# First attention of a two-layer encoder step: where queries and keys are turned and split

## What is computed

```python
h = rmsnorm(x, norm_mix[0])
z = h @ w_in                       # 1024 -> 3 * 1024 + 16
q, k, v = 16 heads of 64 each      # k and v are outputs too
logf = log_sigmoid(z[..., 3072:] + b_f)
cum = cumsum(logf)                 # per head, along the tokens
logits = q @ k.T * 64 ** -0.5 + cum_q[:, None] - cum_k[None, :]
p = softmax(where(mask, logits, NEG))
x = x + (p @ v) @ w_o
x = x + square(relu(rmsnorm(x) @ w_up)) @ w_down
```

## Time and profile before

| | |
|---|---|
| median of 3 runs | 1616.43 us (1614.15 to 1616.51) |
| the profiled execution's own time | 1614.33 us |
| its span in the profile | 1612.5 us |
| PE busy in the span | 1534.1 us, 95% |
| DVE, ACT, POOL busy | 1083.9, 734.0, 411.6 us |
| projection of the first layer | to 195.24 us |
| first attention | 195.24 us to about 372 us |

### The profile page before, as it was taken

One profiled execution on the slowest core, in us unless ns is written; L12 is line 12 of the kernel. 1 busy time (PEld: TensorE's weight loads), 2 busy tenths in 40 slices (PEclk: granted clock), 3 DMA queues, 4 the chain that ended last, 5 costly groups with the idle time before them and its releaser, 6 DMA issues.

```text
span 1612.5 us, 30906 instructions
## 1 busy us (share of the span) xinstructions
PE 1534.1 (95%) x10817; PEld 1447.4 (90%) x10817; DVE 1083.9 (67%) x1997; ACT 734.0 (46%) x1528; POOL 411.6 (26%) x435
## 2 busy tenths in 40 slices
PE   7999889999899999999988897999989999999997
PEld 6777679989899999999988686999888999999997
DVE  5221067875987777787674246788598878778775
ACT  5232157774443434334253434777444433434434
POOL 0010045552332222122000003455343222212200
PEclk9999979999999999999999898999999999999998
DMA  8253531200222312313230537221012322321311
GB/s 286 93 188 90 158 98 40 63 27 27 77 73 87 104 54 102 104 52 104 71 113 2 205 130 213 67 66 33 27 52 79 105 82 75 104 97 59 104 52 60
DMA packets 127780, 146.06 MB, mean 91 GB/s; under 512 B 17776, under 2 KB 103984, under 8 KB 127712
## 3 DMA queue, kind: packets, MB, share of 16 engines
q1 hardware_dynamic: 127712, 145.16, 28.2%
HBM read 120.54 MB, written 24.60 MB: 90 GB/s over the span
## 4 chain that ended last, share of the span: by engine, by line
PE 81%; issue 7%; DVE 6%; ACT 3%; DMA 1%; POOL 1%; SPq 0%; POOLq 0%; ACTq 0%; DVEq 0%
PE ps L2058 25%; PE ps L1745 23%; PE ps L2089 20%; PE ps L1916 3%; PE ps L1960 2%; PE ps L1961 2%; PE ps L1962 2%; PE ps L1931 1%; PE ps L1887 1%; PE ps L1939 1%; DVE wul L1471 1%; DVE wul L1266 1%; PE ps L1909 1%; DVE bl L1517 1%; DVE xT L1500 1%
## 5 line engine op out<-in xcount | busy, mean ns | idle before, releaser
L1569 DVE TENSOR_TENSOR xT<-xT,ps 128x592 f32<-128x592 f32 (+1 forms) x256 | 195.0, 762 | 55.2 <-PE ps L2058 53.3
L2089 PE MATMUL ps<-bh,wuh 128*128 128x296 f32 (+1 forms) x512 | 153.9, 301 | 8.5 <-DVE wul L1471 4.9
L755 POOL TENSOR_TENSOR prob<-prob,rs 128x144 f32<-128x144 f32 (+4 forms) x160 | 118.8, 756 | 140.0 <-DVE rs L1370 140.0
L2089 PE MATMUL ps<-bl,wuh 128*128 128x296 f32 (+1 forms) x512 | 153.6, 300 | 0.0
L2089 PE MATMUL ps<-bh,wul 128*128 128x296 f32 (+1 forms) x512 | 153.3, 299 | 0.0
L1380 DVE TENSOR_TENSOR ptl<-ps,pth 128x256 fp32r<-128x256 f32 (+2 forms) x192 | 95.9, 501 | 66.0 <-ACT pth L989 65.9
L1745 PE MATMUL ps<-wh,xgh 128*128 128x512 f32 (+5 forms) x320 | 123.2, 385 | 4.1 <-DVE zr L1668 3.2
L822 POOL TENSOR_TENSOR ssum<-raw 128x512 f32<-128x512 f32 x32 | 49.2, 1538 | 292.3 <-DMA raw<-in_w_up 289.8
L1745 PE MATMUL ps<-wl,xgh 128*128 128x512 f32 (+5 forms) x320 | 122.0, 381 | 0.0
L1745 PE MATMUL ps<-wh,xgl 128*128 128x512 f32 (+5 forms) x320 | 121.4, 380 | 0.0
L2058 PE MATMUL ps<-hh,dn2h 128*128 128x296 f32 (+1 forms) x512 | 111.3, 299 | 0.0
(11 more groups left out here) (261 smaller groups left out, 4686.6 us busy)
## 6 DMA issues: line engine op xcount, KB each, us to landing
raw<-in_w_up SPq DMA_DIRECT2D x32, 1024.0 KB, 7.1
raw<-in_w_down SPq DMA_DIRECT2D x32, 1024.0 KB, 5.1
raw<-in_w_in_a SPq DMA_DIRECT2D x12, 1024.0 KB, 8.2
kv_mla<-stn SPq DMA_DIRECT2D x24, 256.0 KB, 2.3
raw<-in_w_o_a SPq DMA_DIRECT2D x8, 512.0 KB, 7.1
natk<-kv_mla SPq DMA_DIRECT2D x8, 512.0 KB, 3.6
raw<-in_w_o_b SPq DMA_DIRECT2D x8, 512.0 KB, 7.3
q_mla<-stn SPq DMA_DIRECT2D x16, 192.0 KB, 1.9
```

The costliest lines, as they stand in the source:

```text
L755: g.tensor_tensor(prob[c][0:rows, off:off + n], prob[c][0:rows, off:off + n], rs[0:rows, u:u + 1].to_broadcast([rows, n]), ALU.mult).then_ ...
L1569: v.tensor_tensor(a, a, two_banks(2 + m % 2, n), ALU.add).then_inc(x_ready if last else acc_done, 1)
L2089: i = te.matmul(ps[:, bank, 0:h], w[:, k, :], x, start=(u not in (3, 4, 6) and k == 0 and p == 0), stop=(k == 3 and p == 2), skip_group_ch ...
```

## The change

- Blocks are now only v, v, k, k. Two turned scratch tensors in DRAM take the place of the old ones, with 132 rows a head: 64 rows of high parts, 64 of low parts (for q: high first too; the load takes 128 rows or the last 68), and 4 rows for the running sums and ones, split as well.
- k: while PE goes on with the next tile's product, it turns the k tile just staged (four 128x128 transposes a group, 14 groups with the two cached tiles, placed by `turns`), ACT copies the high part and DVE subtracts for the low part, SP stores four pieces a group.
- The sums are turned once (7 transposes), copied by ACT and stored with 12 transfers; the norm's factor for q is turned once (5 transposes).
- q is computed turned: eight pairs of heads, 48 matmuls of 296 columns each (weights as the stationary side), DVE multiplies with the norm's factor, ACT copies the high part, DVE subtracts, SP stores four pieces a pair.
- SP loads the operands of heads 0 and 1 after the stores of pair 4, w_o after those of pair 5, v of the first two pairs (two buffers now) after those of pair 6 and after PE has finished the projection.
- In the attention every head is loaded by itself with five transfers (`fox_head`) once `scores` of the head two before is done. `prep` and its copies and subtractions are gone. `scores` makes two passes, of 128 rows (high k stacked twice against low and high q) and of 68 rows (low k and the sums).
- The POOL copies of the two columns and the loads and stores of the old scratch tensors are gone. Weight slots of w_in are used in another order, so that slots 1 and 3 come free first.

```diff
-R_FOX, R_MLA = HD + 2, HD + ROPE
+R_FOX, R_MLA = HD + 4, HD + ROPE
+HEAD_ROWS = 2 * HD + 4
...
+        def slot_of(j):
+            return (1, 3, 0, 2)[j % 4] if j < KVD0 else j % 4
...
-        BLOCKS = [("v", 0), ("v", 1), ("k", 0), ("k", 1), ("q", 0), ("q", 1)]
+        BLOCKS = [("v", 0), ("v", 1), ("k", 0), ("k", 1)]
+        def turns(b, t):
+            if (b, t) == (len(BLOCKS), 0):
+                return [(13, 1, NT)]
+            if b not in (2, 3):
+                return []
+            g = 7 * (b - 2)
+            return {0: [(g, b - 2, 5)] if b == 2 else [(g - 1, 0, NT), (g, 1, 5)], 1: [(g + 1, b - 2, 0)], 2: [(g + 2, b - 2, 1)],
+                    3: [(g + 3, b - 2, 2), (g + 4, b - 2, 6)], 4: [(g + 5, b - 2, 3)]}[t]
...
+            def fox_head(h, c):
+                r = h * HEAD_ROWS
+                sp.dma_start(kh[c][0:HD, :].bitcast(F32), kT[bass.ds(r, HD), :]).then_inc(kq_in[c], 16)
+                sp.dma_start(kh[c][HD:P, :].bitcast(F32), kT[bass.ds(r, HD), :]).then_inc(kq_in[c], 16)
+                sp.dma_start(qh[c][:, :].bitcast(F32), qT[bass.ds(r, P), :]).then_inc(kq_in[c], 16)
+                sp.dma_start(kl[c][0:R_FOX, :].bitcast(F32), kT[bass.ds(r + HD, R_FOX), :]).then_inc(kq_in[c], 16)
+                sp.dma_start(ql[c][0:R_FOX, :].bitcast(F32), qT[bass.ds(r + HD, R_FOX), :]).then_inc(kq_in[c], 16)
...
+            for j in range(PAIRS):
+                sp.wait_ge(qt_lo, j + 1)
+                for p in range(2):
+                    for low in range(2):
+                        sp.dma_start(qT3[2 * j + p, HD * (1 - low):HD * (1 - low) + HD, :],
+                                     qst[HD * p:HD * p + HD, j % 3, low, :].bitcast(F32)).then_inc(qt_out[j % 3], 16)
+                if j == 4:
...
+                    fox_head(0, 0)
+                    fox_head(1, 1)
+                if j == 5:
+                    load_wo(0)
+                if j == 6:
...
+                    sp.wait_ge(half_used, KVD0)
+                    fox_v(0, 0)
+                    fox_v(1, 1)
...
+            with sp.Fori(0, PAIRS // 2 - 1) as i:
+                for k in range(2):
+                    for c in range(2):
+                        sp.wait_ge(s_ps, i * 20 + (10 * k + 5 * c + 5))
+                        fox_head(4 * i + (2 * k + c + 2), c)
+                    sp.wait_ge(v_split, i * 2 + (k + 1))
+                    fox_v(2 * i + (k + 2), k)
...
+            for i in range(3):
+                dve.wait_ge(kt_out[i], 64 * len(range(i, 14, 3)))
+            for j in range(PAIRS):
...
+                v.tensor_tensor(halves(qtmp[:, j % 2, :]), two_banks(j % 2, T), halves(rT[:]), ALU.mult).then_inc(q_tmp, 1)
+                dve.wait_ge(qt_hi, j + 1)
+                v.tensor_tensor(qst[:, j % 3, 1, :], qtmp[:, j % 2, :], qst[:, j % 3, 0, :].bitcast(F32),
+                                ALU.subtract).then_inc(qt_lo, 1)
...
+            for j in range(PAIRS):
+                pc = 8 + 2 * (j // 4)
+                if j < 2:
+                    pe.wait_ge(blk_evac, N_BLK)
+                else:
+                    pe.wait_ge(q_tmp, j - 1)
+                for k in range(KD):
...
+                    for p, (w, x) in enumerate(((w_h, xgh), (w_h, xgl), (w_l, xgh))):
+                        for t in range(2):
+                            i = te.matmul(ps[:, 2 * (j % 2) + t, 0:TH], w, x[:, k, TH * t:TH * t + TH],
...
-                    a_h, a_l = qh[c][0:R, q0:q0 + rows], ql[c][0:R, q0:q0 + rows]
+                    if layer == 0:
+                        passes = [(qh[c][:, q0:q0 + rows], kh[c]), (ql[c][0:R, q0:q0 + rows], kl[c][0:R])]
...
-                        if u == 0:
+                        if u == 0 and layer == 0:
+                            pe.wait_ge(kq_in[c], pair * 80 + 80)
+                        elif u == 0:
                             pe.wait_ge(g_lo, qk_split(h) + G0)
                         scores(h, c, u)
-                        if u < 3 and not last:
+                        if layer == 1 and u < 3 and not last:
...
-                pe.wait_ge(nat_qk[0], 80 + 40 * PAIRS * layer)
-                for g in range(3):
-                    prep(-1, g, 0, 0)
+                if layer == 1:
+                    pe.wait_ge(nat_qk[0], 80)
+                    for g in range(3):
+                        prep(-1, g, 0, 0)
```

More of the change, by code:

```diff
@@ L589, in mla_q @@
                 nq = natq[1][slot]
[L590 to L607, removed]
-            fox_v(PAIRS - 1)
+                sp.dma_start(nq[:, 0:NT, :], q_mla[0:SEQ, c].rearrange("(t p) n -> p t n", p=P)).then_inc(nat_qk[slot], 16)
+                sp.dma_start(nq[0:TX, NT, :], q_mla[SEQ:T, c]).then_inc(nat_qk[slot], 16)
             def mlp_loads(layer):
@@ L1010, in step @@
                             out(h - 2, c, pair - 1)
-                        if not last:
+                        if layer == 1 and not last:
                             qk(h, u, 1 - c)
@@ L1022, in step @@
                     exp(h, c, 4)
-                for k in range(3):
+                for k in range(3 * layer):
                     qk(-1, k, 0)
@@ L1027, in attention @@
                 step(1, 1, 0)
+                if layer == 0:
+                    for i in range(3):
+                        act.wait_ge(qt_out[i], 64 * len(range(i, PAIRS, 3)))
+                    for i in range(4):
+                        act.wait_ge(st_out[i], stored(i, N_BLK))
                 with act.Fori(1, PAIRS - 1) as i:
@@ new lines, in _ @@
+            spans = ((slice(0, NT), P), (slice(NT, 5), TX), (slice(5, 7), P))
+            for t, r in spans:
+                if t.start < 5:
+                    v.tensor_copy(aug(t, r, 6), fp[0:r, t, :])
+                i = v.tensor_scalar(aug(t, r, 0), fp[0:r, t, :], -1.0, None, ALU.mult)
+            link(i)
+            for t, r in spans:
+                if t.start < 5:
+                    v.tensor_tensor(aug(t, r, 7), fp[0:r, t, :], aug(t, r, 6).bitcast(F32), ALU.subtract)
+                i = v.scalar_tensor_tensor(aug(t, r, 1), fp[0:r, t, :], -1.0, aug(t, r, 0).bitcast(F32), ALU.mult, ALU.subtract)
@@ new lines, in _, with turned_lo @@
+            i.then_inc(F_ready, 1)
+            lo(6)
+            lo(7)
+            def turned_lo(g, t):
+                dve.wait_ge(kt_hi, g + 1)
+                r = TX if t == NT else P
+                v.tensor_tensor(turned_view(kst[:, g % 3, 1, :], r), turned_view(ps[:, 6 + g % 2, :], r),
+                                turned_view(kst[:, g % 3, 0, :], r).bitcast(F32), ALU.subtract).then_inc(kt_lo, 1)
+            for b in (2, 3):
+                for t in range(5):
+                    for g, f, tt in turns(b, t):
+                        turned_lo(g, tt)
+                    if b == 3 and t == 2:
+                        dve.wait_ge(rq_ps, 1)
+                        v.tensor_copy(rT[:, 0:SEQ], ps[:, 4, :])
+                        v.tensor_copy(rT[:, SEQ:T], ps[:, 5, 0:TX]).then_inc(rq_ready, 1)
+                lo(2 * b + 4)
+                lo(2 * b + 5)
@@ L1413, in step @@
                     recip(h, 1)
-                    if not last:
+                    if layer == 1 and not last:
                         qk(h, 2, 1 - c)
-                    else:
+                    if last:
                         wo_low(layer, 0)
@@ L1884, in scores @@
                         kk = slice(k0 + c0, k0 + c1)
-                        mm(out, a_h, kh[c][0:R, kk], True, False)
+                        mm(out, passes[0][0], passes[0][1][:, kk], True, False)
                         if c1 > mk0:
```

362 lines of the change are left out of this document (213 added, 149 removed).

## The result

| | before | after |
|---|---|---|
| median | 1616.47 us (4 runs, 1614.15 to 1616.96) | 1634.85 us (4 runs, 1629.04 to 1636.59) |
| the profiled execution's own time | 1614.33 us | 1629.04 us |
| its span | 1612.5 us | 1627.2 us |

The changed kernel is slower: ratio 1.011, 95% interval 1.0082 to 1.0138. The forecast was 1610.5 with a range up to 1622, so the sign is wrong and the range did not hold the time.

What follows compares the result with a forecast made beforehand. PE's work seemed the bound, with a 5.03 us handoff chain just beneath it in each head. The terms 4.3 - 1.5 - 8.5 - 0.2 gave -5.9, so a median of 1610.5 us, range 1604 to 1622.

Steps and rivals of the forecast that it cites:

- Turning k: Projection: PE's added transposes and the last copy cost 7.5 us (6 to 11), so the q part starts at 147.1.
- q in eight pairs: Projection's q part: 296-column matmuls start 0.137 apart, 52.6 us against 55.6; the 3 us gained are worth nothing by themselves.
- The way to head 1: Start to head 1's first turn: v lands late behind w_o, turn at 221.7 against 217.39, +4.3 us (0 to +10).
- Rival 1: 68-row loads of heads are served by few DMA engines, delaying w_o and v: 1617 us; chance 0.28.
- Head 1: Head 1's step, at the lower clock at first, loses three preps: -1.5 us (-0.6 to -3).
- Heads 2 to 14: Thirteen first-layer heads: a step falls from 9.77 to 9.12 us, 0.65 a head, -8.5 in all (-4 to -11).
- the 5.03 us: In each head, the handoff chain from `p_turn` 1 over ACT and DVE to `scores` 4, said to stay unchanged.
- Head 15: Head 15's step, which had no turns of q or k: only the saved passes count, -0.2 us.
- Loads in the loop: Each head's five loads take 4.7 to 9.8 us and fit in 10.5 us of room, so no cost.
- Rival 3: Slower: PE waits for a head's loads ahead of `scores` 0; 1624.5 us at a load time of 12.5; chance 0.16.
- rival 2: PE's work is the heads' bound after all: 7.7 us a head, -27 over 13 heads, 1592 us; chance 0.06.
- The rest: w_o, out projection, MLP and second attention: the same instructions, so no change in time.

Runs made afterwards that it cites:

- e3_filler: Changed kernel plus eight unread matmuls of 336 columns ahead of `scores` 4 in first-layer heads from head 1 on: 1617.13 us, ratio 1.0006.
- e4_max_first: Changed kernel with DVE taking the row maxima of tiles 1 and 2 ahead of its subtractions, first layer: 1611.92 us, ratio 0.9969.
- e10_no_split: Changed kernel with w_o loaded after pair 1's stores and maxima before DVE's subtractions, 68-row loads left whole: 1603.12 us, ratio 0.9906.

## Why the prediction was wrong, point by point

*Turning k.* Right. The q part starts at 147.01 (forecast 147.1). A small stall behind it I had not seen: DVE stands 4.36 us ahead of its first product for q, until k's stores have landed, and PE's third pair starts at 160.98, 0.8 us later than 147.01 + 2 x 6.57.

*q in eight pairs.* Right: rows of two matmuls of 296 columns start 0.27 apart:

```profile
147.66 0.43 PE L2012 MATMUL ps<-xgh,wl 128*128 128x296 f32 x2
147.93 0.44 PE L2012 MATMUL ps<-xgh,wh 128*128 128x296 f32 x2
148.21 0.43 PE L2012 MATMUL ps<-xgl,wh 128*128 128x296 f32 x2
```

*The way to head 1: +4.3 forecast, +12.9 measured.* This is the first step that failed. The outline held: operands issued at 185.95 (forecast 185.0), v behind w_o in one queue, POOL's two splits behind v, the turn behind them. The sum failed at "At 308 GB/s from 39.4 on, the heads are in at 46.7": it priced all ten operand loads at that one rate. Two in five of them have 68 rows and go slower, and w_o then took 19.0 us to issue instead of the 13.9 that I had for landing: its last issue ended at 213.71, where I had it landed at 209.7. That is 4.0 of the 8.7 us by which v was late (222.3, not 213.6). With the split, w_o's issues end at 210.03, close to my figure, and v still lands 4.9 us late. So the other half is a second term of the same sum, "pair 6's stores at 64.6, and only then v of pair 0, at 66.5": 3.9 us from the end of w_o to v's landing, priced by bytes, as if SP had issued all of it ahead. SP was held until w_o's last issue was through. Only then it issued the stores (3.6 us) and v's four loads (2.2), and the last of these landed 3.0 after its issue began: 8.56 us without the split, 8.47 with it. The trace of before already had a row for this, SP held by w_o's eight issues:

```profile
168.65 11.60 SPq L520 DMA_DIRECT2D raw<-in_w_o_a  x8
```

Rival 1, which I gave 0.28 and a price of "7 us later at most", thus has the mechanism of the first half only. That 8.7 were measured is near its price by luck: splitting the 68-row loads gave back 3.8. (From 37.9, where the issues of pair 4's stores end, to the 39.4 of the sum I gave no row either; SP's next issue came at 185.95, 38.9 in that count.)

*Head 1: -1.5.* Right.

*Heads 2 to 14: -8.5 forecast, +2.4 measured.* The second step that failed, and only one sentence of it: "PE's clock holds: a stretch with 8.19 busy of 10 was granted 1.00". The reading of the 5.03 us was exact, the wait ahead of `scores` 4 was 1.54 where I had 1.4, and the two heads at full clock took 8.80 and 9.23 where I had 9.12. But seven heads of thirteen were longer, 10.36 and more, and e3_filler shows that this is the clock's doing: filled, the same heads take 8.97. The row I leaned on proves nothing either way: the changed kernel itself shows 8.46 us busy of 10 at 1.00 and again at 0.84 (where matmuls at the lower clock count longer, so that there is less work in it):

```profile
290.00:300.00 10.00, 8.46 (x85) 8.18 (x83) 6.24 (x18) 6.42 (x18) 5.17 (x7) 1.00 0.48 137
306.00:316.00 10.00, 8.46 (x67) 8.21 (x66) 5.48 (x15) 5.49 (x17) 4.60 (x6) 0.84 0.38 113
```

*Head 15: -0.2.* Right.

*Loads in the loop: nothing.* Nearly right, by luck (and 2.5 and 2.0 are 4.5, not the 4.7 of the sum, which changes nothing): the five loads of head 3 took 10.9 us (237.87 to 248.77 in the chain; `ql` alone landed 8.45 after its issue), beyond the 9.8 that was my far end, and only the long heads hid that (0.7 us of waits in all). Where heads became short the loads were waited for (e4_max_first, e10_no_split). Rival 3, which had the slower sign, so did not decide it; rival 2 is excluded, as the heads were never 7.7 while the 5.03 stood.

*The rest: nothing forecast, +1.0 measured.* From the turn of the last head to the end the instructions are the same in all twelve kernels, and their profiles have 1244.7 to 1252.5 us for them. So 1.0 is nothing, and single spans compare badly: that is why the table above counts to the last head's turn.

The two failed steps make 8.6 and 10.9 of the 20.6 us between the forecast's -5.9 and the profile's +14.7, the rest of the kernel 1.0.

## What to carry to other kernels

When an edit takes work from the engine that seems to be the bound, look for the chain of handoffs beneath it and shorten that as well: here removing 23 us of PE's work brought nothing by itself, and two DVE instructions that changed places brought 23 us. Idle time that such an edit opens in every round is not free even where the chain sets the end, because the clock may fall on the work behind it; price a repeated wait once at either level. And write down what each transfer's row count is, and what is queued behind it in the same queue: 68 rows against 64 and 4 was worth 10 to 16 us, and w_o placed ahead of v another 10. Price the issuing engine's own time as well, since what stands behind a held issue in its program starts late whatever its bytes.

## What the runs showed of the hardware

- The granted clock fell to 0.50 after a PE wait of 1.54 us and stayed there through some 3 us of unbroken work. With a like wait in each head it fell in some heads and stayed at 1.00 in two (heads 6 and 7); what tells them apart no run shows. Extra matmuls in the wait held it at 1.00 over 125 us.
- Issuing is not always 0.5 us: the eight issues of w_o (4.19 MB) kept SP for 11.6 us in the kernel before and for 12.4, 13.3 or 19.0 in the changed ones, and all that stands behind in SP's program waited with it.
- The same bytes took less of the queue's time as 64 and 4 rows than as 68, in spite of one more issue a load: w_o's issues behind them took 13.3 us, not 19.0, and from 200 to 205 us the queue moved 301 GB/s, not 176.
- The second layer and the MLPs, the same instructions in every kernel here, took between 1244.7 and 1252.5 us from one profile to the next.
